# First loads in another order: the context behind the first projection's weights, the constants in three parts, the context's norm beside the first projections

## The reference, cut to what matters

```python
def rmsnorm(x, w):
    y = xf * rsqrt(mean(xf * xf) + EPS)
    return y * w
mod_lat = silu(c) @ w_ada + b_ada          # for the 256 tokens x
mod_ctx = silu(c_ctx) @ w_ada + b_ada      # for the 256 tokens of the context
l_* = mixer_inputs(modulate(rmsnorm(x, attn_norm_w), sa, sca), w_in, ..., ang)
c_* = mixer_inputs(modulate(rmsnorm(ctx, attn_norm_w), csa, csca), w_in, ..., None)
dk_all = concatenate([c_dk, l_dk]);  ...   # keys and values: context, then x
o_diff = softmax(dq @ dk_all) ...;  o_mla = ...
```

## Time and profile before

| what | us |
|---|---|
| median of three runs | 1910.37 (1909.67 to 1911.39) |
| the profiled execution | 1913.46 |
| its span, first to last instruction | 1911.7 |
| PE busy | 1717.5, 90% of the span |
| mean granted clock of TensorE | 0.955 of full speed |
| DMA traffic | 547 MB, mean 286 GB/s |

### The profile page before, as it was taken

How to read it: one execution, slowest core, us unless ns; L and a number is a source line. 1 busy time by engine, 2 the same in 40 slices (tenths; PEclk the granted TensorE clock), 3 DMA queues, 4 the chain that set the end, 5 groups by cost and what they waited for, 6 DMA issues and landing times.

```text
span 1911.7 us, 20785 instructions
## 1 busy us (share of the span) xinstructions
PE 1717.5 (90%) x8428; PEld 1042.1 (55%) x8428; DVE 445.7 (23%) x1017; ACT 279.5 (15%) x572; POOL 118.5 (6%) x261
## 2 busy tenths in 40 slices
PE   6996999779985989688988889899998999999997
PEld 3633585334441434133433234377776788888886
DVE  4224322111120122011112111235556412121101
ACT  4013412110010111010101001022323300100000
POOL 2871000000000000000000000000030000000000
PEclk9998999989998999799999999999999999999999
DMA  9425657999999999999999999963443335534250
GB/s 373 159 87 201 224 215 301 415 416 400 419 420 418 414 416 419 421 416 411 418 422 416 414 419 417 411 247 111 154 170 111 110 103 195 180 118 176 95 191 23
DMA packets 135730, 547.03 MB, mean 286 GB/s; under 512 B 9982, under 2 KB 23434, under 8 KB 99659
## 3 DMA queue, kind: packets, MB, share of 16 engines
q1 hardware_dynamic: 129248, 529.83, 70.0%
q0 software_dynamic: 3200, 11.01, 1.5%
q10 hardware_dynamic: 3178, 4.78, 0.7%
HBM read 540.33 MB, written 7.62 MB: 287 GB/s over the span
## 4 chain that ended last, share of the span: by engine, by line
PE 56%; DMA 14%; SPq 11%; DVE 2%; issue 1%; ACT 0%; DVEq 0%
PE PS L1267 12%; SPq L1639 9%; PE PS L2198 8%; DMA ring<-in_w 7%; DMA arena<-in_w 7%; PE PS L1293 5%; PE PS L2039 4%; PE PS L2224 4%; PE PS L2060 3%; PE PS L1243 3%; PE PS L1304 3%; PE PS L2052 2%; PE PS L2046 2%; PE PS L2188 1%; PE PS L2068 1%; SPq L1633 1%
## 5 line engine op out<-in xcount | busy, mean ns | idle before, releaser
L1267 PE MATMUL PS<-ring,arena 128*32 128x512 f32 (+2 forms) x1088 | 269.5, 661 | 58.1 <-DMA ring<-in_w 32.3
L1267 PE MATMUL PS<-arena 128*64 128x512 f32 (+2 forms) x960 | 246.2, 676 | 37.0 <-DMA arena<-in_w 23.6
L1267 PEld LDWEIGHTS PS<-ring,arena 128*32 128x32 f32 (+2 forms) x1088 | 84.2, 140 | 206.3 <-issue 205.9
L1267 PEld LDWEIGHTS PS<-arena 128*64 128x64 f32 (+2 forms) x960 | 74.5, 141 | 160.1 <-issue 160.0
L2198 PE MATMUL PS<-arena,ring 128*128 128x256 f32 x704 | 152.6, 379 | 0.0
L1533 DVE TENSOR_SCALAR arena<-PS 128x512 f32<-128x512 f32 x28 | 19.2, 686 | 556.0 <-PE PS L1277 556.0
L2198 PEld LDWEIGHTS PS<-arena,ring 128*128 128x128 f32 x704 | 133.5, 190 | 18.0
L1293 PE MATMUL PS<-arena 128*32 128x512 f32 (+2 forms) x512 | 121.1, 641 | 20.9 <-DMA arena<-in_w 19.5
L1293 PE MATMUL PS<-ring,arena 128*32 128x512 f32 (+2 forms) x512 | 115.6, 607 | 17.0 <-DMA ring<-in_w 13.9
L1399 ACT ACTIVATE arena<-arena 128x512 f32<-128x512 f32 x28 | 17.6, 630 | 492.5 <-DVE arena L1533 492.5
L1293 PEld LDWEIGHTS PS<-arena 128*32 128x32 f32 (+2 forms) x512 | 38.7, 136 | 90.5 <-issue 90.5
(11 more groups left out here) (454 smaller groups left out, 1946.1 us busy)
## 6 DMA issues: line engine op xcount, KB each, us to landing
ring<-in_w SPq DMA_DIRECT2D x200, 1024.0 KB, 22.5
arena<-in_w SPq DMA_DIRECT2D x184, 1024.0 KB, 23.1
ring<-in_w_ada SPq DMA_DIRECT2D x24, 1024.0 KB, 7.6
ring<-in_w_in SPq DMA_DIRECT2D x22, 1024.0 KB, 13.9
ring<-in_w_up SPq DMA_DIRECT2D x20, 1024.0 KB, 7.6
ring<-in_w_gate SPq DMA_DIRECT2D x16, 1024.0 KB, 7.1
ring<-in_w_down SPq DMA_DIRECT2D x11, 1024.0 KB, 8.4
ring<-in_w_out SPq DMA_DIRECT2D x8, 1024.0 KB, 5.2
```

Source lines behind the costliest of these rows:

```text
L1267: m = pe.matmul(bank(("up", i, b))[rows[n], :], xs[:, k, rows[n]], tiles[n][:, b * 512:(b + 1) * 512], start=k == 0, stop=False, skip_grou ...
```

## The change

The context's load goes behind the first ten loads of the list (w_ada and dq's weights). The table of constants is laid out anew, so that `rot`, `cos` and `sin` follow the first 256 columns; ACT's second load of constants takes these 640 columns only, and a third load, issued in the step `dk 1`, takes the rest (2304 columns), for whose readers three new waits for `more_in` stand in the routing and the second block. The context's norm leaves its place ahead of `mrow`: ACT squares all eight slabs of the context behind `h 0` into the context's half of `hT`, which is still unused, so that no slab waits for one of the two `sqb` buffers. PE's sum, the root, the reciprocal and `h 1` come behind the step `dq 1` and its following rope step.

```diff
--- before.py
+++ after.py
@@ -32,8 +32,8 @@
                      ("b1", 512), ("pscale", 4), ("s5_are", 16), ("s5_aim", 16), ("s5_ldt", 16), ("s5_d", 4)])
-CST_N = _table(CST, [("ident", 128), ("ones", 128), ("rot", 128), ("tri", 128), ("before", 128), ("iota", 2 * S), ("cos", 256), ("sin", 256),
-                     ("m01", 384), ("mneg", 384), ("inv", 1024), ("eps", 1)])
+CST_N = _table(CST, [("ident", 128), ("ones", 128), ("rot", 128), ("cos", 256), ("sin", 256), ("m01", 384), ("mneg", 384), ("inv", 1024),
+                     ("tri", 128), ("before", 128), ("iota", 2 * S), ("eps", 1)])
 
@@ -211,7 +211,7 @@
         par_in, squares_in, eps_set, cst_in = sem("par_in"), sem("ident_ones_in"), sem("eps_set"), sem("cst_in")
-        ctx_in, x_in = sem("ctx_in"), sem("x_in")
+        ctx_in, x_in, more_in = sem("ctx_in"), sem("x_in"), sem("more_of_cst_in")
         silu_e, c2_zero, c2_ready = sem("silu_e"), sem("c2_zero"), sem("c2_ready")
@@ -279,8 +279,8 @@
 
-        PRE = [("silu",)] + [("phase", i) for i in range(8)] + [("power", k) for k in range(7)] + [("b1t", q) for q in range(4)] + [("rms", "x"), ("rms", "ctx")]
-        PRE += [("mrow", 0, k) for k in range(8)] + [("mcol", 0), ("aw",), ("h", 0), ("h", 1)]
+        PRE = [("silu",)] + [("phase", i) for i in range(8)] + [("power", k) for k in range(7)] + [("b1t", q) for q in range(4)] + [("rms", "x")]
+        PRE += [("mrow", 0, k) for k in range(8)] + [("mcol", 0), ("aw",), ("h", 0), ("ctxsquare",)]
         late = []
@@ -291,6 +291,8 @@
             dense(("dq", j), True)
+            if j == 1:
+                PRE += [("rms", "ctx"), ("h", 1)]
         for j in range(4):
@@ -505,7 +507,7 @@
                         w.wait_ge(sq_ready, q + k + 1)
-                        i = pe.matmul(psum(s, 0, n), ones, sqb[(q + k) % 2][:, 0:n], start=k == 0, stop=k == K - 1, skip_group_check=True)
+                        i = pe.matmul(psum(s, 0, n), ones, hT[:, k, 0:256] if s[1] == "ctx" else sqb[(q + k) % 2][:, 0:n], start=k == 0, stop=k == K - 1, skip_group_check=True)
                         i.then_inc(sq_spent, 1)
@@ -678,7 +680,7 @@
             act.dma_start(par[:, :], I["par"]).then_inc(par_in, 16)
-            e0 = CST["eps"][0]
+            e0 = CST["sin"][1]
             act.dma_start(cst[:, 0:256], I["cst"][:, 0:256]).then_inc(squares_in, 16)
@@ -745,19 +747,21 @@
                     act.activation(subr, psum(s, 0, 8), ACT.Sqrt, scale=1.0 / 128, bias=eps).then_inc(moved[g.bank], 1)
+                elif kind == "ctxsquare":
+                    w.wait_ge(ctx_in, 16)
+                    for k in range(8):
+                        act.activation(hT[:, k, 0:256], ctxT[:, k, :], ACT.Square).then_inc(sq_ready, 1)
                 elif kind == "rms":
...
                         w.wait_ge(x_in, 16)
-                    elif key == "ctx":
-                        w.wait_ge(ctx_in, 16)
                     elif key == "cq":
...
                         w.wait_ge(moved[G["ckv",].bank], G["ckv",].use)
-                    for k in range(K):
+                    for k in range(0 if key == "ctx" else K):
                         if q + k >= 2:
@@ -775,6 +779,8 @@
                     r = raw[2 * i % 3]
+                    if s == ("dk", 1):
+                        act.dma_start(cst[:, CST["m01"][0]:CST["iota"][1]], I["cst"][:, CST["m01"][0]:CST["iota"][1]]).then_inc(more_in, 16)
                     w.wait_ge(pe_done, g.n)
@@ -1204,6 +1210,7 @@
                     i.then_inc(pe_done, 1)
+            w.wait_ge(more_in, 16)
             w.wait_ge(mask_ready, 1)
@@ -2777,8 +2786,9 @@
             sp.dma_start(xv, I["xT"].rearrange("(k p) t -> p k t", p=128)).then_inc(x_in, 16)
+            load_all(sp, w, plan.loads[:10], pe_done, slot_in)
             sp.dma_start(ctxT, I["ctxT"].rearrange("(k p) t -> p k t", p=128)).then_inc(ctx_in, 16)
-            load_all(sp, w, plan.loads[:MAIN_LOADS], pe_done, slot_in)
+            load_all(sp, w, plan.loads[10:MAIN_LOADS], pe_done, slot_in)
             w.wait_ge(most_ready, 1)
```

## The result

The changed kernel is slower: 1919.72 us (1917.86 to 1928.21, 5 runs) against 1910.64 of the kernel before, ratio 1.0057 (95% interval 1.0043 to 1.0070). Forecast were 1912.0 and a range that ended at 1916.

What follows compares the result with a forecast made beforehand. DMA pace first, then PE without gaps from 57.51 to 144.35, then a wait for ACT, DVE and POOL's tables. PE's gain is lost there: -0.5 + 2.1 = +1.6 us on 1910.37 gives 1912.0, range 1908 to 1916.

Steps and rivals of the forecast that it cites:

- Its mechanism: First softmax step: PE gains 4.2 to 4.5 us, spent waiting for POOL's tables, which start 8.8 us late.
- +1.6: Whole kernel: forecast change in us, from 0.5 gained at qr's first rotation and 2.1 lost to the slow clock.
- The head: Start of the stage: earlier loads let dq 0 start at 33.9 and dk 0 at 53.3, 4.2 us sooner.
- the gap of 0.9 us: Before the first rotation: PE stands from 40.7 to 41.6, waiting for dq 0's copy behind ACT's squares.
- my second rival: First projections: PE's clock at a half, tables 2.4 us later, +4.0 us in all, 1914.4; chance 0.16.
- The last store is issued at 157.8: POOL's tables: start at 51.6 plus 106.2 us; landing in 3.8 us puts them there at 161.6.
- the 106.2 us: POOL's tables: time from first step to last store's issue, three landings of 3.7 to 3.8 included, taken as unchanged.
- My own upper bound: First softmax step: tables at 166.3 at the latest, which makes the change +6 us.
- the 165 that I had named as the sign of being wrong: First softmax step: forecast at 161 to 162, declared wrong if before 157 or after 165.
- The clock behind the long wait: First rotation of qr: after PE idles 7 to 8 us, 5.5 us at the slow pace cost 2.1.
- at 153 or before: ACT's exponential ahead of the first softmax step: expected by 153 instead of 157.12, after its long DMA issues.
- My sentence that POOL's rounds show little of the shared ports: POOL's tables: 106.2 us hold whichever DVE work lies beside, so shared SBUF ports add nothing to the sum.

Runs made afterwards that it cites:

- e3: Kernel before, with POOL's tables held back until dq 2's product is done: 1916.52 us, ratio 1.0033.
- e12: Changed kernel with the context's load back in second place, three-part constants and moved norm kept: 1926.07 us, ratio 1.0068.
- e11: Kernel before with the constants' part of the change alone (new layout, 320 KB at first, rest later): 1910.75 us, ratio 0.9992.
- e7: Changed kernel as it is, run again for a second profile: 1921.62 us, ratio 1.0059.
- e4: Changed kernel with two w_ada loads of SP's queue held until dv 0 is done: 1922.69 us, ratio 1.0062.
- e5: Changed kernel; POOL does six doublings of its first table round from h_ready 8 on, the rest from 16: 1913.87 us, ratio 1.0007.
- e9: As e5, with ACT's two router loads also moved behind kn 3: 1912.4 us, ratio 1.0003.
- e10: Kernel before with only ACT's two router loads moved behind kn 3: 1911.63 us, ratio 1.0002.
- e1: Changed kernel with POOL's tables started at h_ready 8 instead of 16: 1917.85 us, ratio 1.0041.
- e2: Kernel before with POOL's tables started at h_ready 8 instead of 16: 1913.6 us, ratio 1.0018.
- e16: Kernel before with POOL's tables begun at 18 us and ACT's router loads behind kn 3: 1907.72 us, ratio 0.9985.
- e15: Changed kernel with POOL's tables begun at 18 us, router loads left in place: 1913.36 us, ratio 1.0010.

## Why the prediction was wrong

Its mechanism held: the tables, at most 2.6 us early before, start some 10 us late and take the place of the wait that the change shortens; e3 alone shows 6.2 us from this, e12 against e11 that the norm's place causes it. The direction was right, the size not: +1.6 against +9.1, 7.5 us missing. In the first pair of profiles they split into a later start of the tables (1.25), the store that met two loads (3.85) and the clock behind the wait (2.4).

- The head, dq 0 at 33.9 (34.04) and dk 0 at 53.3 (54.24): right but for 0.9, and in part by luck. PE's clock fell at about 27 while it waited for slab after slab (0.83 in the stretch 25 to 28), so dq 0 began at the half clock and dq 1 ended 1.9 us late, at 42.6; the gap of 0.9 us that I had put before the first rotation was not there and took back half of it. This is my second rival's mechanism, which I gave 0.16; it was in both profiles of the changed kernel. I had priced it at 2.4 us of the tables' start; `h_ready` 16 came at 52.85 (53.7 in e7) instead of 51.6, so it cost 1.25 and 2.1.
- "The last store is issued at 157.8" is the step that failed: it was issued at 162.92. I carried the 106.2 us of the earlier trace rows over, with three landings of 3.7 to 3.8. From the new start they were 110.1: the second store, at 104.74, met the pair of w_ada loads that PE's gain had moved from 109.0 to 105.7, and landed in 7.5 us instead of 3.8. The earlier trace rows had the warning, 8.5 us beside another transfer; I used it for the last store alone and priced it out. Start and collision make 5.1 of the 7.5 us missing in the profiles; in the medians only the start is shown, by e3, since e4 without the collision was no faster.
- The bounds. My own upper bound, tables at 166.3 and +6 us, gives 1916.4; I then wrote 1914.0 as the forecast's upper end and drew the range from that. The tables' last store landed at 166.67, and the first softmax step, at 166.69, passed the 165 that I had named as the sign of being wrong.
- The clock behind the long wait: predicted +2.1, measured +4.5 in the first profile (19.1 less 14.6), +1.8 in e7. I took 5.5 us at the slow pace, with 0.43 us from row to row; it was slow for 9.6 us, from 170.96 to 180.6, and the eight rows that took 3.97 us followed each other every 0.49.
- ACT's issues: "at 153 or before" was right (152.0), but this was no free slack. In e5, e9 and e10 one holder replaces the other; all else was ready 5 us early only while the tables' store kept out of the copy.
- My sentence that POOL's rounds show little of the shared ports looked at one side only: DVE pays (7.50 instead of 3.26 in e1), and POOL's first product too where h 1 was already under way (2.31 instead of 0.20 in e2).

Open are e2's 3.3 us and e4's missing gain: both lie in the medians, and their profiles up to the routing do not show them. Not tried: tables in two buffers, which would take the stores' landings out of POOL's chain.

## What to carry to other kernels

When a step moves, look for who starts on its signal, even an engine off the path: here a counter of the context's half started POOL's tables, and their last store was 2.6 us ahead of the path in one profile and 0.5 behind it in another. Put every transfer of that side chain on the new time axis against every other queue; its duration at the old place does not carry over. And do the parts singly: a smaller second load of constants gave the whole gain at dk 0 (and still no time, until the next holders moved), the moved norm only its price.

## What the runs showed of the hardware

- The second of two 512 KB stores that POOL issues 0.6 us apart took 3.7 to 3.8 us to land when no other queue was busy. Beside two 1 MB loads of SP's queue it took 7.5 to 7.7 (after, e7, e12), beside ACT's copy of 2304 KB 8.2 to 11.1 (8.5 before, 8.2 in e9, 11.1 in e16).
- ACT's issue of the 128 KB router load, and of the few bytes of router_b behind it, took 0.39 and 0.46 us in e9 at 174.5 us, but 6.84 and 3.92 in the changed kernel, right behind the copy to skew_scratch on the same queue, and up to 10.54 (e1) and 7.61 (e15) when a store of POOL's ran beside it. ACT computed nothing meanwhile (idle from 139.1 to 153.8 in e5).
- Eight DVE operations with two SBUF inputs took 3.26 us alone and 7.50 beside POOL's products (e1).
- TensorE's granted clock fell from full to a half at about 27.0 us in the changed kernel. PE had been at work without a gap until 22.5, then for 1.1 us from 22.91 and again from 25.41; the longest idle time was 1.4 us. In e7, the same kernel, it fell at 25.2, in e5 at 30.0.
- Behind a wait of 9.4 us (after) PE ran at the half clock for 9.6 us of work without a gap before it got the full one, behind 8.5 us (e7) for 3.9, behind 15 us (before) for 5.4.
